# Attention's output projection by token halves, with five of its groups in the last slots of attention, and gating by halves

## The chip, the cores and the metric

One core of a Trainium2 chip runs the kernel. The metric is device time in microseconds (us) of one execution; the time before is a median of three runs.

## What is computed

Two transformer layers in fp32, on 1024 tokens of width 1024. The change lies in the first layer, between its attention and the product with `w_out`:

```
att = sliding_window_attention(aq, ak, av, sinks)          # (S, 512), 8 heads of 64
ret = retention_chunkwise(rq, rk, rv)                      # (S, 1024), 4 heads of 256
ret = head_group_norm(ret, gain) * silu(rg)                # "gating"
merged = sigmoid(ga) * (att @ w_att_o) + sigmoid(gr) * (ret @ w_ret_o)
x = x + merged @ w_out
```

## The kernel before

Each engine has a program of its own, written out by hand: `pe_program` (TensorE), `act_program` (ScalarE), `dve_program` (VectorE), `pool_program` (GpSimd), and a program of the SP queue that issues all DMAs. An engine works its instructions in that order; the order between engines comes from semaphores. Every fp32 operand of a large product is split in two parts, high (H) and low (L), and a product of 128 rows is three matmuls (WL by H, WH by L, WH by H; lines 597 to 599). Weights arrive in `WRAW` (three buffers), ScalarE writes the high part `WH`, VectorE or GpSimd the low part `WL` (lines 979, 1428, 2094), in seven slots. A weight tile is split in `feed(key)` once the last group that reads the slot's earlier tile is done, and SP fetches a tile once the one three before it has been split. The eight PSUM banks go round in the order in which TensorE opens them (`Banks.take`).

The stage has four parts.

1. The slot loop (line 776, 37 slots, s = 0 to 36). Retention has 32 turns `R1` (chunk t = 0 to 7, four heads), attention 32 turns `A1` (t = 0 to 7, four pairs of heads), each spread over several slots. TensorE's slot s holds, for attention turn a = s - 2: scores of a (line 749), values of a - 3 (line 761), the turning of the probabilities of a - 2 (line 772), and for retention scores of s, values of s - 1 (line 723), turning of s - 3 (line 738). Retention's turns end at slot 34, attention's scores at slot 33, its last values (turn 31) stand in slot 36. Between two steps of one turn the other engines work: VectorE adds the bias and takes the maximum (line 1602), ScalarE takes the exponential (1092), VectorE sums and inverts (1586, 1589), ScalarE and GpSimd scale, ScalarE copies the turned probabilities to `PT` (1112). The result of turn q goes to `ATH` (ScalarE, 1103) and `ATL` (VectorE, 1628), 128 features by 128 tokens. Tokens 0 to 511 (half 0) are complete with turn 15, tokens 512 to 1023 (half 1) with turn 31.
2. `ao`, attention's output projection (lines 791 to 794): 16 groups (n, half), n = 0 to 7 feature tiles, half = 0, 1 token halves, 12 matmuls of 128x512 each, ordered (0,0), (0,1), (1,0), ... It starts after the last turn's ATL. VectorE multiplies a group by its gate `TA` into `TB` (line 1645) and SP stores that to DRAM (2615).
3. The gating, one step beside each `ao` group: VectorE multiplies retention's output in `QK` by gain and gate `RG` (1638), ScalarE writes its high part `RH` (1132), GpSimd its low part `RL` (2212). SP loads the gates (2600, 2603).
4. `ro2`, retention's output projection (`RO2`, line 466), 16 groups of 24 matmuls. TensorE waits for RL of (7, half) before a group of that half. VectorE multiplies by the second gate and adds the stored `ao` group, both loaded in `MG` (2625, 2626; 1655, 1658). Then comes `out`, the product with `w_out`.

Of the kernel before, what the change touches and what calls it, by code (L numbers as in the profile page):

```python
# [147 lines left out]
def build(nc, a, out):  # L148
# [75 lines left out]
    TA = at("TA", [P, 2, S], MI + 18)  # L224
    RG = at("RG", [P, 4, 512], MI + 9.5)
    TB = at("TB", [P, 2, 512], MI + 5.5)
# [218 lines left out]

    def queries_in(t):

        return c.at(("lg0", "lg1", "lm0", "lm0")[t] if t < 4 else "lm1", "aq")
# [13 lines left out]
    LAG_A = 2  # L462
    A2 = [(h, i) for h in range(8) for i in range(NT)]
    OPEN = [(j, 0, 256) for j in range(4)] + [(j, 256, 256) for j in range(4)] + [(j, 512, 512) for j in range(4)]

    RO2 = [(n, half) for n in range(6) for half in range(2)] + [(n, half) for half in range(2) for n in range(6, 8)]
# [114 lines left out]
    def pe_program(e):  # L581
# [192 lines left out]

        nr, n1 = len(R1), len(A1)
        for s in range(n1 + LAG_A + 3):
            a = s - LAG_A
            if s < nr:
                ret_scores(s)
            if 0 <= a < n1:  # L780
                att_scores(a)
            if 0 <= s - 1 < nr:
                ret_values(s - 1)
            if 0 <= a - 3 < n1:
                att_values(a - 3)
            if 0 <= a - 2 < n1:
                att_turn(a - 2)
            if 0 <= s - 3 < nr:
                ret_turn(s - 3)

        w.wait_ge(*bk.out(("apv", n1 - 1)))
        for n in range(8):
            for half in range(2):
                proj_t(("ao", n, half), U["u_ao", n // 2], half, ATH, ATL, 4, (n % 2) * 512)
# [165 lines left out]
    def act_program(e):  # L960
# [168 lines left out]
        for i in range(16):  # L1129
            j, half = i // 2, i % 2  # L1130
            w.wait_ge(*c.at("rg_m", i))
            e.activation(RH[:, j, hs(half)], QK[:, j, hs(half)], ACT.Copy).then_inc(*c.inc("rg_h", (j, half)))
            feed(("ao", j, half))
# [283 lines left out]
    def dve_program(e):  # L1417
# [140 lines left out]

        nr, n1 = len(R1), len(A1)
# [4 lines left out]
        for s in range(n1 + LAG_A + 3):  # L1564
# [59 lines left out]
            if 0 <= q < n1:  # L1624
# [4 lines left out]
                                ATH[:, 2 * g + jp, blk(t)].bitcast(F32), ALU.subtract).then_inc(*bk.free(key))  # L1629
            if s == 3:  # L1630
                feed(("P3", 0, NB0 - 1, 0))
# [3 lines left out]
        for i in range(16):  # L1635
            n, half = i // 2, i % 2
            w.wait_ge(*c.at(f"lga{i % 4}", ("rg", i)))
            e.scalar_tensor_tensor(out=QK[:, n, hs(half)], in0=QK[:, n, hs(half)], scalar=GAIN[:, n:n + 1],
                                   in1=RG[:, i % 4, :], op0=ALU.mult, op1=ALU.mult).then_inc(*c.inc("rg_m", i))
            key = "ao", n, half  # L1640
            w.wait_ge(*bk.full(key))
            w.wait_ge(*c.at(f"lg{n % 2}", ("ga", n)))
            if i >= 2:
                w.wait_ge(*c.at(f"m1_{i % 2}", i - 2))
            e.tensor_tensor(TB[:, i % 2, :], PS[:, bk.at(key), :], TA[:, n % 2, hs(half)],
                            ALU.mult).then_inc(*bk.free(key))
            feed(key)
# [435 lines left out]
    def pool_program(e):  # L2083
# [125 lines left out]
        for i in range(16):  # L2209
            j, half = i // 2, i % 2  # L2210
# [3 lines left out]
            feed(("ao", j, half))  # L2214
# [215 lines left out]
    def sync_program(e):  # L2430
# [168 lines left out]
        def load_ga(n):  # L2599
            e.dma_start(TA[:, n % 2, :], scr_gx[n]).then_inc(*c.inc(f"lg{n % 2}", ("ga", n), 16))  # L2600

        def load_rg(i):
            e.dma_start(RG[:, i % 4, :], scr_rg[i // 2][:, hs(i % 2)]).then_inc(*c.inc(f"lga{i % 4}", ("rg", i), 16))

        stored0(NB0 - 1)
        w.wait_ge(*bk.out(("ro", len(R1) - 1)))
        for i in range(4):
            load_rg(i)
        w.wait_ge(*bk.out(("as", len(A1) - 1)))
        for n in range(2):  # L2610
            load_ga(n)
        for i in range(16):
            n, half = i // 2, i % 2
            w.wait_ge(*bk.out(("ao", n, half)))
            e.dma_start(scr_ga[n][:, hs(half)], TB[:, i % 2, :]).then_inc(*c.inc(f"m1_{i % 2}", i, 16))
            if half == 1 and n + 2 < 8:
                load_ga(n + 2)
            if i + 4 < 16:
                w.wait_ge(*c.at("rg_m", i))
                load_rg(i + 4)  # L2620
            feed(("ao", n, half))
# [390 lines left out]
```

## Time and profile before

| | us |
|---|---|
| median of 3 runs | 2707.33 (2704.08 to 2710.63) |
| the profiled execution, its own time | 2689.97 |
| its span, first to last instruction | 2688.2 |
| the span less TensorE's busy time | 57.3 |
| slot loop | 496 to 647 |
| `ao` and gating | 647 to 690.6 |
| `ro2` | 690.6 to 777.7 |

Times within the span are those of one profiled execution, on a clock that starts with its first instruction. A row of a timeline gives the start, the time from the first start to the last end of the merged instructions, engine, line and operands; in brackets stands the idle time of the engine before it and what ended it. Matmuls overlap, so their cost is read from start to start. The granted clock of TensorE (PEclk) is a share of 2.4 GHz.

### The profile page before, as it was taken

The page shows a single profiled execution, that of the slowest core. Times are in us where ns is not written, and L with a number is a line of the kernel's source. Part 1 is how long each engine was busy: PE and PEld are TensorE (multiplying, and loading weights), DVE is VectorE, ACT ScalarE, POOL GpSimd, SP SyncE. Part 2 cuts the span into 40 slices and gives each one's busy share as a digit, 9 for nine tenths or more (in the row PEclk, how much of TensorE's full clock was granted, in tenths as well). Part 3 has the DMA queues.
Part 4 walks back from the last instruction along what each step waited for, and adds up shares of the span by engine and source line. Part 5 has one row for each costly group of instructions (what it writes and reads, how often), then busy time and mean ns, then how long its engine had stood idle before and what let it go on. Part 6 is the DMA issues. An engine that isn't in the chain of part 4 may idle for free.

```text
span 2688.2 us, 35515 instructions
## 1 busy us (share of the span) xinstructions
PE 2630.9 (98%) x13170; PEld 2205.8 (82%) x13170; DVE 1548.2 (58%) x2628; ACT 1027.8 (38%) x2053; POOL 1179.5 (44%) x936
## 2 busy tenths in 40 slices
PE   7999999899999999999999999999999999999998
PEld 7788888677888988888888778989988888878886
DVE  4325555575434644554698641167647666668787
ACT  4122333475212423332444531057634322244443
POOL 2347878344425655565231763334234444300205
PEclk9999999899999999999999999999999999999999
DMA  4545766803542222222753344233043333273524
GB/s 169 181 184 204 266 228 249 305 1 122 199 169 90 79 86 79 79 86 71 274 184 99 114 153 142 74 69 65 20 141 100 104 114 106 95 257 133 188 95 164
DMA packets 161993, 372.35 MB, mean 139 GB/s; under 512 B 21365, under 2 KB 41973, under 8 KB 158197
## 3 DMA queue, kind: packets, MB, share of 16 engines
q1 hardware_dynamic: 161822, 370.08, 40.2%
q8 instruction: 106, 1.74, 0.3%
q14 instruction: 65, 0.53, 0.1%
HBM read 267.94 MB, written 101.83 MB: 138 GB/s over the span
## 4 chain that ended last, share of the span: by engine, by line
PE 88%; DVE 4%; POOL 2%; DMA 2%; ACT 2%; issue 1%; SPq 0%; POOLq 0%; DVEq 0%; ACTq 0%
PE PS L696 12%; PE PS L698 12%; PE PS L699 12%; PE PS L829 5%; PE PS L830 5%; PE PS L831 5%; PE PS L613 4%; PE PS L615 4%; PE PS L614 4%; PE PS L930 3%; PE PS L597 3%; PE PS L598 3%; PE PS L599 3%; PE PS L908 1%; PE PS L749 1%
## 5 line engine op out<-in xcount | busy, mean ns | idle before, releaser
L2094 POOL TENSOR_TENSOR WL<-WRAW,WH 128x512 fp32r<-128x512 f32 (+1 forms) x149 | 253.0, 1698 | 395.0 <-ACT WH L979 395.0
L696 PE MATMUL PS<-HH,WL 128*128 128x512 f32 (+1 forms) x928 | 349.0, 376 | 5.3 <-DVE HS L1736 3.1
L699 PE MATMUL PS<-HH,WH 128*128 128x512 f32 (+1 forms) x928 | 347.7, 375 | 0.0
L698 PE MATMUL PS<-HL,WH 128*128 128x512 f32 (+1 forms) x928 | 347.7, 375 | 0.0
L1428 DVE TENSOR_TENSOR WL<-TS,WH 128x512 fp32r<-128x512 f32 x216 | 227.5, 1062 | 182.9 <-ACT WH L979 182.8
L829 PE MATMUL PS<-WH,DAL 128*128 128x512 f32 x756 | 295.7, 391 | 5.5 <-DVE WL L1694 5.5
L830 PE MATMUL PS<-WL,DAH 128*128 128x512 f32 x756 | 294.7, 390 | 0.0
L831 PE MATMUL PS<-WH,DAH 128*128 128x512 f32 x756 | 294.6, 390 | 0.0
L2280 POOL TENSOR_TENSOR X<-X,DV 128x512 f32<-128x512 f32 x56 | 90.1, 1634 | 357.9 <-DVE DV L1806 275.3
L979 ACT ACTIVATE WH<-TS 128x512 fp32r<-128x512 f32 x216 | 130.9, 623 | 199.5 <-POOL TS L2110 199.4
L696 PEld LDWEIGHTS PS<-HH,WL 128*128 128x128 f32 x928 | 174.8, 188 | 37.1 <-DVE HS L1736 3.3
L613 PE MATMUL PS<-WH,HL 128*128 128x512 f32 x512 | 203.2, 397 | 1.2 <-DVE HL L1973 0.9
L699 PEld LDWEIGHTS PS<-HH,WH 128*128 128x128 f32 x928 | 174.9, 188 | 31.3
L698 PEld LDWEIGHTS PS<-HL,WH 128*128 128x128 f32 x928 | 174.9, 188 | 31.1
L615 PE MATMUL PS<-WH,HH 128*128 128x512 f32 x512 | 200.2, 391 | 0.0
L2110 POOL TENSOR_TENSOR TS<-WRAW 128x512 f32<-128x512 f32 x108 | 144.8, 1341 | 126.3 <-issue 122.8
L614 PE MATMUL PS<-WL,HH 128*128 128x512 f32 x512 | 199.9, 390 | 0.0
L979 ACT ACTIVATE WH<-WRAW 128x512 fp32r<-128x512 f32 (+1 forms) x236 | 175.4, 756 | 56.3 <-PE PS L615 18.7
L1428 DVE TENSOR_TENSOR WL<-WRAW,WH 128x512 fp32r<-128x512 f32 (+1 forms) x87 | 112.3, 1291 | 109.5 <-ACT WH L979 109.4
L829 PEld LDWEIGHTS PS<-WH,DAL 128*128 128x128 f32 x756 | 142.3, 188 | 37.8 <-issue 5.8
L1694 DVE TENSOR_TENSOR WL<-WRAW,WH 128x512 fp32r<-128x512 f32 x189 | 155.2, 821 | 23.6 <-ACT WH L1174 23.6
L831 PEld LDWEIGHTS PS<-WH,DAH 128*128 128x128 f32 x756 | 142.3, 188 | 29.4
(366 smaller groups left out, 6145.1 us busy)
## 6 DMA issues: line engine op xcount, KB each, us to landing
WRAW<-in_u_f SPq DMA_DIRECT2D x56, 512.0 KB, 3.6
WRAW<-in_u_in SPq DMA_DIRECT2D x54, 512.0 KB, 4.4
WRAW<-scr_t SPq DMA_DIRECT2D x52, 512.0 KB, 3.7
scr_h<-HS SPq DMA_DIRECT2D x96, 256.0 KB, 2.2
WRAW<-in_u_gu SPq DMA_DIRECT2D x44, 512.0 KB, 3.5
scr_t<-TTa SPq DMA_DIRECT2D x19, 1024.0 KB, 4.4
WRAW<-in_u_out SPq DMA_DIRECT2D x24, 512.0 KB, 3.5
scr_x<-X SPq DMA_DIRECT2D x24, 512.0 KB, 5.0
```

Source lines behind the costliest of these rows:

```text
L613: e.matmul(PS[:, b, :], HL[:, k, ts], whole_slot(WH, n)[:, cs], start=(k == 0), stop=False)
L614: e.matmul(PS[:, b, :], HH[:, k, ts], whole_slot(WL, n)[:, cs], start=False, stop=False)
L615: mm = e.matmul(PS[:, b, :], HH[:, k, ts], whole_slot(WH, n)[:, cs], start=False, stop=(k == 7))
L696: e.matmul(PS[:, b, 0:wd], wl[:, blk(kk)], op_moving(q, kk, c0, wd, 0), start=(kk == 0), stop=False)
L698: e.matmul(PS[:, b, 0:wd], wh[:, blk(kk)], op_moving(q, kk, c0, wd, 1), start=False, stop=False)
L699: mm = e.matmul(PS[:, b, 0:wd], wh[:, blk(kk)], op_moving(q, kk, c0, wd, 0), start=False, stop=(kk == 3))
L829: e.matmul(dst, hl, wh, start=(i == 0), stop=False)
L830: e.matmul(dst, hh, wl, start=False, stop=False)
L831: mm = e.matmul(dst, hh, wh, start=False, stop=(i == g - 1))
L979: e.activation(dst, src, ACT.Copy).then_inc(*c.inc("w_hi", i))
L1428: e.tensor_tensor(lo, raw, hi.bitcast(F32), ALU.subtract).then_inc(*c.inc("w_lo_v", i))
L2094: e.tensor_tensor(lo, raw, hi.bitcast(F32), ALU.subtract).then_inc(*c.inc("w_lo_p", i))
```

## The change

- `ao` is ordered by halves (`AOG`): all eight n of half 0, then all eight of half 1. Its first five groups (`N_TAIL` = 5), all of half 0, stand at the end of slots 32 to 36 of the slot loop, in TensorE's program and in VectorE's (the multiplication by the gate, after ATL). The other eleven follow the loop, after the same wait for the last ATL.
- The gating goes by halves too (`GATED`: j = 0 to 7 of half 0, then of half 1), still 16 steps; the first eleven stand beside `ao` groups 5 to 15, the last five alone.
- `ro2` takes n = 0 to 5 of half 0, then n = 0 to 5 of half 1 (before: both halves of each n); its last four groups are as before.
- The gate tiles of `ao` are now eight buffers of one half each: four in the place of `RV`'s chunks 4 and 5, loaded once retention's turn 23 is done, four in the place of `TA`. SP loads them one per group (16 of 256 KB, before 8 of 512 KB). Two of `RG`'s four buffers and `TB` lie in other places, and SP's loads of `RG` and its waits follow from that.

```diff
--- before.py
+++ after.py
@@ -221,9 +221,10 @@
     SM = at("SM", [P, 256], MI + 0.5)
     AB = at("AB", [P, 8, 256], MI + 18)
     FA = [at("FAa", [P, 512], MI + 13.5), at("FAb", [P, 512], MI + 15.5)]
-    TA = at("TA", [P, 2, S], MI + 18)
-    RG = at("RG", [P, 4, 512], MI + 9.5)
-    TB = at("TB", [P, 2, 512], MI + 5.5)
+    TA = ([at(f"TAa{i}", [P, 512], B2 + 16 + 2 * i) for i in range(4)]
+          + [at(f"TAb{i}", [P, 512], MI + 18 + 2 * i) for i in range(4)])
+    RG = [at(f"RG{i}", [P, 512], MI + kb) for i, kb in enumerate((9.5, 11.5, 1.5, 3.5))]
+    TB = at("TB", [P, 2, 512], MI + 13.5)
     MG = at("MG", [P, 2, 2, 512], MI + 1.5)
     RKN = at("RKN", [P, 2, P], MI + 1.5)
     STM = at("STM", [P, 2, P], MI + 2.5)
@@ -443,6 +444,13 @@
         base, scr = {0: (14, scr_qk), 1: (6, scr_gx), 2: (22, scr_rg), 3: (30, scr_gr)}[m // 4]
         return scr[tile - base][:, hs(int(q[0]) - 1)]
 
+    def gate_at(i):
+
+        return TA[i if i < 4 else 4 + i % 4]
+
+    def gate_in(i):
+        return c.at(("lg0", "lg1", "lm0", "lm1")[i % 4], ("ga", i))
+
     def queries_in(t):
 
         return c.at(("lg0", "lg1", "lm0", "lm0")[t] if t < 4 else "lm1", "aq")
@@ -460,10 +468,13 @@
     A1 = [(t, g, jp) for t in range(NT) for g in range(2) for jp in range(2)]
     R1 = [(t, h) for t in range(NT) for h in range(4)]
     LAG_A = 2
+    N_TAIL = LAG_A + 3
+    AOG = [(n, half) for half in range(2) for n in range(8)]
     A2 = [(h, i) for h in range(8) for i in range(NT)]
     OPEN = [(j, 0, 256) for j in range(4)] + [(j, 256, 256) for j in range(4)] + [(j, 512, 512) for j in range(4)]
 
-    RO2 = [(n, half) for n in range(6) for half in range(2)] + [(n, half) for half in range(2) for n in range(6, 8)]
+    GATED = [(j, half) for half in range(2) for j in range(8)]
+    RO2 = [(n, half) for half in range(2) for n in range(6)] + [(n, half) for half in range(2) for n in range(6, 8)]
     PO = [0, 4, 1, 5, 2, 6, 3, 7]
     OUTS = ([(0, tt) for tt in PO[:4]] + [(1, tt) for tt in PO[:4]] + [(1, tt) for tt in PO[4:]]
             + [(0, tt) for tt in PO[4:]])
@@ -772,6 +783,11 @@
                     mm = e.transpose(PS[:, b, blk(2 * e2 + kb)], PB[:, q % 3, e2, blk(kb)], ID[:, :])
             mm.then_inc(*bk.fill(("at", q)))
 
+        def att_out(i):
+            n, half = AOG[i]
+            w.wait_ge(*bk.out(("apv", n1 - 1 if half else n1 // 2 - 1)))
+            proj_t(("ao", n, half), U["u_ao", n // 2], half, ATH, ATL, 4, (n % 2) * 512)
+
         nr, n1 = len(R1), len(A1)
         for s in range(n1 + LAG_A + 3):
             a = s - LAG_A
@@ -787,11 +803,12 @@
                 att_turn(a - 2)
             if 0 <= s - 3 < nr:
                 ret_turn(s - 3)
+            if s >= n1:
+                att_out(s - n1)
 
         w.wait_ge(*bk.out(("apv", n1 - 1)))
-        for n in range(8):
-            for half in range(2):
-                proj_t(("ao", n, half), U["u_ao", n // 2], half, ATH, ATL, 4, (n % 2) * 512)
+        for i in range(N_TAIL, 16):
+            att_out(i)
         for n, half in RO2:
             w.wait_ge(*c.at("rg_l", (7, half)))
             proj_t(("ro2", n, half), U["u_ro", n], half, RH, RL)
@@ -1127,10 +1144,11 @@
 
         w.wait_ge(*bk.out(("ro", nr - 1)))
         for i in range(16):
-            j, half = i // 2, i % 2
+            j, half = GATED[i]
             w.wait_ge(*c.at("rg_m", i))
             e.activation(RH[:, j, hs(half)], QK[:, j, hs(half)], ACT.Copy).then_inc(*c.inc("rg_h", (j, half)))
-            feed(("ao", j, half))
+            if i + N_TAIL < 16:
+                feed(("ao", *AOG[i + N_TAIL]))
         for i, (n, half) in enumerate(RO2):
             w.wait_ge(*c.at("mg_a", i))
             e.activation(HH[:, n, hs(half)], MR[:, i % 2, :], ACT.Copy).then_inc(*c.inc("mg_h", (n, half)))
@@ -1555,6 +1573,18 @@
                     n_split[0] += 1
                 else:
                     feed(BEHIND[key][0])
+
+        def att_out(i):
+
+            key = "ao", *AOG[i]
+            w.wait_ge(*bk.full(key))
+            w.wait_ge(*gate_in(i))
+            if i < 2:
+                w.wait_ge(*bk.out(("rs", nr - 1)))
+                w.wait_ge(*c.at("r_q", nr - 1))
+            else:
+                w.wait_ge(*c.at(f"m1_{i % 2}", i - 2))
+            e.tensor_tensor(TB[:, i % 2, :], PS[:, bk.at(key), :], gate_at(i)[:, :], ALU.mult).then_inc(*bk.free(key))
 
         nr, n1 = len(R1), len(A1)
         w.wait_ge(*c.at("small", "all"))
@@ -1627,24 +1657,21 @@
                 w.wait_ge(*c.at("a_hi", q))
                 e.tensor_tensor(ATL[:, 2 * g + jp, blk(t)], PS[:, bk.at(key), 0:128],
                                 ATH[:, 2 * g + jp, blk(t)].bitcast(F32), ALU.subtract).then_inc(*bk.free(key))
+            if s >= n1:
+                att_out(s - n1)
             if s == 3:
                 feed(("P3", 0, NB0 - 1, 0))
 
         w.wait_ge(*bk.out(("rot", nr - 1)))
         w.wait_ge(*bk.full(("apv", n1 - 1)))
         for i in range(16):
-            n, half = i // 2, i % 2
+            n, half = GATED[i]
             w.wait_ge(*c.at(f"lga{i % 4}", ("rg", i)))
             e.scalar_tensor_tensor(out=QK[:, n, hs(half)], in0=QK[:, n, hs(half)], scalar=GAIN[:, n:n + 1],
-                                   in1=RG[:, i % 4, :], op0=ALU.mult, op1=ALU.mult).then_inc(*c.inc("rg_m", i))
-            key = "ao", n, half
-            w.wait_ge(*bk.full(key))
-            w.wait_ge(*c.at(f"lg{n % 2}", ("ga", n)))
-            if i >= 2:
-                w.wait_ge(*c.at(f"m1_{i % 2}", i - 2))
-            e.tensor_tensor(TB[:, i % 2, :], PS[:, bk.at(key), :], TA[:, n % 2, hs(half)],
-                            ALU.mult).then_inc(*bk.free(key))
-            feed(key)
+                                   in1=RG[i % 4][:, :], op0=ALU.mult, op1=ALU.mult).then_inc(*c.inc("rg_m", i))
+            if i + N_TAIL < 16:
+                att_out(i + N_TAIL)
+                feed(("ao", *AOG[i + N_TAIL]))
         for i, (n, half) in enumerate(RO2):
             key = "ro2", n, half
             w.wait_ge(*bk.full(key))
@@ -2207,11 +2234,12 @@
                 feed(("P3", 0, NB0 - 1, 0))
 
         for i in range(16):
-            j, half = i // 2, i % 2
+            j, half = GATED[i]
             w.wait_ge(*c.at("rg_h", (j, half)))
             e.tensor_tensor(RL[:, j, hs(half)], QK[:, j, hs(half)], RH[:, j, hs(half)].bitcast(F32),
                             ALU.subtract).then_inc(*c.inc("rg_l", (j, half)))
-            feed(("ao", j, half))
+            if i + N_TAIL < 16:
+                feed(("ao", *AOG[i + N_TAIL]))
         for i, (n, half) in enumerate(RO2):
             w.wait_ge(*c.at("mg_h", (n, half)))
             e.tensor_tensor(HL[:, n, hs(half)], MR[:, i % 2, :], HH[:, n, hs(half)].bitcast(F32),
@@ -2596,29 +2624,44 @@
             load_rv(t)
         feed(("P3", 0, NB0 - 1, 0))
 
-        def load_ga(n):
-            e.dma_start(TA[:, n % 2, :], scr_gx[n]).then_inc(*c.inc(f"lg{n % 2}", ("ga", n), 16))
+        def load_ga(i):
+            n, half = AOG[i]
+            e.dma_start(gate_at(i)[:, :], scr_gx[n][:, hs(half)]).then_inc(
+                *c.inc(("lg0", "lg1", "lm0", "lm1")[i % 4], ("ga", i), 16))
 
         def load_rg(i):
-            e.dma_start(RG[:, i % 4, :], scr_rg[i // 2][:, hs(i % 2)]).then_inc(*c.inc(f"lga{i % 4}", ("rg", i), 16))
-
+            j, half = GATED[i]
+            e.dma_start(RG[i % 4][:, :], scr_rg[j][:, hs(half)]).then_inc(*c.inc(f"lga{i % 4}", ("rg", i), 16))
+
+        nr, n1 = len(R1), len(A1)
         stored0(NB0 - 1)
-        w.wait_ge(*bk.out(("ro", len(R1) - 1)))
+        w.wait_ge(*bk.full(("ro", 4 * 5 + 3)))
+        w.wait_ge(*bk.full(("rst", 4 * 5 + 3)))
         for i in range(4):
-            load_rg(i)
-        w.wait_ge(*bk.out(("as", len(A1) - 1)))
-        for n in range(2):
-            load_ga(n)
+            load_ga(i)
         for i in range(16):
-            n, half = i // 2, i % 2
+            if i == 1:
+                w.wait_ge(*bk.full(("ro", nr - 1)))
+                load_rg(0)
+                load_rg(1)
+            if i == 3:
+                w.wait_ge(*bk.full(("rot", nr - 1)))
+                load_rg(2)
+                load_rg(3)
+            n, half = AOG[i]
             w.wait_ge(*bk.out(("ao", n, half)))
             e.dma_start(scr_ga[n][:, hs(half)], TB[:, i % 2, :]).then_inc(*c.inc(f"m1_{i % 2}", i, 16))
-            if half == 1 and n + 2 < 8:
-                load_ga(n + 2)
             if i + 4 < 16:
-                w.wait_ge(*c.at("rg_m", i))
-                load_rg(i + 4)
-            feed(("ao", n, half))
+                w.wait_ge(*bk.out(("as", n1 - 1)))
+                load_ga(i + 4)
+            if i >= N_TAIL:
+                if i - N_TAIL + 4 < 16:
+                    w.wait_ge(*c.at("rg_m", i - N_TAIL))
+                    load_rg(i - N_TAIL + 4)
+                feed(("ao", n, half))
+        for i in range(16 - N_TAIL, 12):
+            w.wait_ge(*c.at("rg_m", i))
+            load_rg(i + 4)
 
         def load_mg(i):
             n, half = RO2[i]
```

## Rows read from the trace of the kernel before

**Rows 1.** The page: span, and busy time of each engine with its share.

```profile
span 2688.2 us, 35515 instructions
PE 2630.9 (98%) x13170; PEld 2205.8 (82%) x13170; DVE 1548.2 (58%) x2628; ACT 1027.8 (38%) x2053; POOL 1179.5 (44%) x936
```

**Rows 2.** Busy time by stretch: length, five engines, PEclk, DMA share, GB/s.

```profile
600.00:630.00 30.00, 30.00 (x194) 21.89 (x193) 21.35 (x82) 23.17 (x81) 15.21 (x29) 1.00 0.01 2
637.20:647.00 9.80, 5.88 (x54) 4.12 (x53) 3.31 (x15) 6.52 (x21) 3.00 (x4) 1.00 0.63 214
647.00:690.60 43.60, 43.60 (x192) 36.12 (x193) 26.90 (x33) 12.74 (x19) 23.24 (x16) 1.00 0.79 268
690.60:720.00 29.40, 29.40 (x131) 24.34 (x130) 9.43 (x12) 6.35 (x9) 11.63 (x7) 1.00 0.49 163
...
750.00:777.00 27.00, 27.00 (x121) 22.34 (x120) 8.39 (x11) 5.07 (x7) 8.80 (x6) 1.00 0.37 117
```

**Rows 3.** Timeline of TensorE, slots 33 to 36 and the first `ao` matmul.

```profile
637.15 1.13 PE L749 MATMUL PS<-AK,AQ 64*128 64x256 f32 x4
...
639.29 0.38 PE L738 MATMUL PS<-ID,ON 128*128 128x128 f32 x2
641.56 0.66 PE L761 MATMUL PS<-PTb,AV 128*64 128x128 f32 x8 [1.88 <-ACT PTb L1112]
...
642.64 0.38 PE L738 MATMUL PS<-ID,ON 128*128 128x128 f32 x2
643.59 0.66 PE L761 MATMUL PS<-PTa,AV 128*64 128x128 f32 x8 [0.56 <-ACT PTa L1112]
644.18 0.66 PE L772 MATMUL PS<-ID,PB 128*128 128x128 f32 x4
645.61 0.66 PE L761 MATMUL PS<-PTb,AV 128*64 128x128 f32 x8 [0.78 <-ACT PTb L1112]
646.97 0.50 PE L597 MATMUL PS<-ATH,WL 128*128 128x512 f32 x1 [0.69 <-DVE ATL L1628]
```

**Rows 4.** Timeline of TensorE, second `ao` matmul, and where `ro2` begins.

```profile
647.31 0.39 PE L598 MATMUL PS<-ATL,WH 128*128 128x512 f32 x1
...
690.63 0.39 PE L597 MATMUL PS<-RH,WL 128*128 128x512 f32 x1
```

**Rows 5.** Timeline of VectorE and ScalarE around slot 33, and VectorE's first gate product.

```profile
637.62 0.54 DVE L1580 TENSOR_SCALAR ON<-PS,RS 128x256 f32<-128x256 f32 x1
638.79 0.48 DVE L1602 CUSTOM_DVE_ANT_0 PB<-PS,AB,SM 128x256 f32<-128x256 f32 x1
...
650.03 0.69 DVE L1645 TENSOR_TENSOR TB<-PS,TA 128x512 f32<-128x512 f32 x1 [2.45 <-PE PS L599]
```

**Rows 6.** Groups by line, 647 to 690.6 (POOL, DVE, ACT): count | busy, mean ns.

```profile
L2212 POOL TENSOR_TENSOR RL<-QK,RH 128x512 fp32r<-128x512 f32 x15 | 20.5, 1374 | 24.1 <-ACT RH L1132 24.1
L2094 POOL TENSOR_TENSOR WL<-WRAW,WH 128x1024 fp32r<-128x1024 f32 x1 | 2.9, 2857 | 0.0
...
L1645 DVE TENSOR_TENSOR TB<-PS,TA 128x512 f32<-128x512 f32 x15 | 10.4, 690 | 15.4 <-PE PS L599 11.0 <-DMA scr_m<-TB 4.4
L1428 DVE TENSOR_TENSOR WL<-WRAW,WH 128x1024 fp32r<-128x1024 f32 x2 | 2.7, 1348 | 1.1 <-ACT WH L979 1.1
...
L1132 ACT ACTIVATE RH<-QK 128x512 fp32r<-128x512 f32 x16 | 10.1, 633 | 30.5 <-DVE QK L1638 30.5
L979 ACT ACTIVATE WH<-WRAW 128x1024 fp32r<-128x1024 f32 x3 | 3.2, 1056 | 0.8 <-PE PS L599 0.7
```

**Rows 7.** Tile RG: the gating product (min/median/max ns), and its loads' time to landing.

```profile
L1638 DVE SCALAR_TENSOR_TENSOR QK<-QK,SM,RG x16: 735/744/1805, 646.8 to 689.4; 128x512 f32<-128x512 f32 x16
...
DMA to landing us min/median/max: 2.8/4.4/6.1
```

**Rows 8.** Tile MG: `ro2`'s first product (first and last start), and its waits.

```profile
L1655 DVE TENSOR_TENSOR MR<-PS,MG x16: 691/692/693, 700.3 to 777.9; 128x512 f32<-128x512 f32 x16
...
DMA MG<-scr_m: 8.8, 1
```

## The prediction, made before the changed kernel was run

> **What bounds the kernel now.** I read the page first: TensorE is busy 2630.9 us of a span of 2688.2, so all that it does not do at once is 57.3 us [rows 1]. Then the stretches around the change: TensorE is busy for the whole of each from 600 to 777 us, at granted clock 1.00, but for one, 637.2 to 647.0, where it is busy 5.88 of 9.80 us [rows 2]. Its timeline names that idle time: 1.88, 0.56 and 0.78 us before the values of slots 34, 35 and 36, each ended by ScalarE's copy of the turned probabilities, and 0.69 us before the first `ao` matmul, ended by ATL of the last turn [rows 3]. Together 3.91 us. These slots hold only what drains: a few small matmuls and the way round the other engines. After them `ao` and `ro2` run without an idle moment, 16 groups of `ao` in 690.63 - 646.97 = 43.66 us, 2.73 us each [rows 3, 4].
>
> So TensorE bounds this stage, and a change can give back here at most the 3.91 us in the drain.
>
> **Part by part.**
>
> *Five groups into the drain.* No matmul is added or removed: 16 groups of 12 before and after. Five groups are 5 x 2.73 = 13.6 us of work put between the small steps. Half 0 needs turns 0 to 15 only, done long before, and the weights of `ao` are split near the loop's start. I lay TensorE's queue out. Slot 32 ends where the scores of slot 33 began, 637.15 [rows 3]. Group 0 runs to 639.9. The small matmuls of slot 33 took 637.15 to 639.67 (2.5 us), those of slot 34 641.56 to 643.02 (1.5), those of slot 35 643.59 to 644.84 (1.25), those of slot 36 645.61 to 646.27 (0.66) [rows 3]. That gives: slot 33 to 642.4, group 1 to 645.1; slot 34 to 646.6, group 2 to 649.3; slot 35 to 650.6, group 3 to 653.3; slot 36 to 654.0, group 4 to 656.7; then eleven groups, 30.0 us, to 686.7. Before it was 690.63. The difference is the 3.91 us, if no group makes a new wait.
>
> *What the groups push back on the other engines.* VectorE's product with the gate stands in its queue after ATL and waits for the whole group; behind it wait the next slot's normalisation, sum and maximum, and for these ScalarE's exponential and PT copy, and for that the next values on TensorE. Slot 33 is the tight one, as it still has a maximum to take. A gate product started 3.06 us after its group's first matmul (650.03 against 646.97) and takes 0.69 [rows 3, 5], so it is done at 637.15 + 3.06 + 0.69 = 640.9. From the start of the normalisation to the end of the second maximum VectorE took 637.62 to 639.27, 1.65 us [rows 5]: done at 642.55. From there to the values of slot 34 the old trace took 641.56 - 639.27 = 2.29 us [rows 3, 5], so they can start at 644.85. TensorE's queue reaches them at 645.1. A cover of 0.25 us: free by my count, and if the count is off, a stall of some tenths. Without that cover the delay of the chain, 3.3 us, would be seen in full; it is hidden by group 1. The later slots have no maximum, and group 2 or 3 (2.73 us) lies ahead of each values step, against ways round of 0.6 to 0.8 us more than TensorE's own work [rows 3]: hidden. The last ATL now has group 4 before its reader, so its 0.69 us goes too. PSUM banks return after eight openings; the closest is the turning of slot 33, which needs the bank that the normalisation of the same slot frees at about 641.4, and TensorE is there at about 642.2.
>
> *The price of alternating.* No row shows a large group between small ones. From below: nothing. From above, two rows: the first matmul of `ao` was 0.34 us ahead of the second where later ones are 0.227 apart (43.66 / 192), a head of 0.11 us [rows 3, 4]; five heads in place of one cost 0.45. The way back, from a group to small matmuls, has no row; as the same head, twice as dear, it would be 4 x 0.23 = 0.9. A gain below nothing is excluded, since nothing is taken away but waits. I take 0.45, as the head is a row of these very instructions, and keep 0 to 1.4.
>
> *Gating by halves.* Its instructions are the same in number and size. It starts after group 4's product, at about 657.7 instead of 646.8, and goes one step a group. `ro2` then asks at 686.7 for RL of (7, 0), the eighth step. Step 7 stands in VectorE's queue behind the product of group 11 (group's end 656.7 + 7 x 2.73 = 675.8, plus the lag of 0.33 and 0.69: 676.8). Then 0.74 for the step [rows 7], 0.63 for RH and 1.37 for RL [rows 6]: 679.5. Two weight splits come in between, as a tile of `w_att_o` now comes free only with its group of half 1: `w_ret_o` tile 3 after group 9 (ScalarE 1.06, VectorE 1.35), which the two groups' slack takes up, and tile 4 after group 11 (ScalarE 1.06, GpSimd 2.86) [rows 6]. Both the latter stand before RH and RL of step 7, so RL comes at 676.1 + 1.06 + 0.63 of RH of step 6 + 2.86 + 1.37 = 682.0 to 682.5. TensorE asks at 686.7: a cover of some 4 us, nothing paid.
>
> *The tail of the gating.* The last five steps run after `ao`. SP's last RG load waits behind the store of group 15 and the fetch that needs tile 6 split (group 15's end 686.7, then 1.06 + 0.63 + 1.37 + 2.86, about 692.5). Landing takes 4.4 us [rows 7], so step 15 is at 697 and the MG loads, which wait for it, land near 702.5, against 700.3 for the first product before [rows 8]. `ro2`'s first group is full at 692.2, so two groups lie in PSUM while six banks are free: nothing on TensorE, which before passed 9 us of the same waiting of VectorE without a gap [rows 2, 8]. RL of (7, 1) is wanted at 686.7 + 6 x 5.44 = 719 and comes near 700.
>
> *`ro2` by halves.* The groups of `ro2` take 5.44 us each (sixteen from 690.6 to 777.7). A new tile is wanted every 5.44 us instead of every 10.9 for the first six. Tiles 0 to 2 are there before; 3, 4, 5 are asked for at 703, 708 and 714 and are split by 673, 681 and 684. Tile 7's slot comes free after `ro2` group 6 (724.8) and is wanted at 757; the first `w_out` tiles' slots after groups 7 to 10, 730 to 747, and are wanted at 773.8. All hidden.
>
> *SP and DMA.* Eight more gate loads of half the size, two issues of 0.43 us and a store of 0.32 in each 2.73 us; the bytes are the same. Four of the loads now fall where DMA is at 0.01 [rows 2]. No cost. The stretch of `ao` and gating had a DMA share of 0.79 and is now shorter by 10 us with some of its loads ahead of it.
>
> **The sum.** 3.91 - 0.45 = 3.5 us less. The profiled execution took 2689.97, with 1.8 us around its span; it would be 2686.5 (span 2684.7). It lies 17.4 us under the median of the runs, so I carry the difference over, not the ratio: 2707.33 - 3.5 = 2703.8 us. Ends: 3.9 with no price, 2.3 with heads both ways and 0.3 of stall in slot 33.
>
> **Rivals.**
>
> 1. *The waits stay, in new places.* VectorE's queue makes TensorE wait in slots 33 to 35. The cover of 0.25 us in slot 33 speaks for it, the 2.73 us in the others against. If every slot lost 0.6 us, 2 to 3 us of the gain would go: about 2706.5.
> 2. *Slower: `ro2` waits for the gating's eighth step.* Its low part comes 4.2 us before TensorE asks, and every us beyond that is lost. The mechanism is there: the gating product took 0.74 us alone but up to 1.81 beside GpSimd [rows 7], 1.07 more. If each of the steps 0 to 7 lost that one after the other, 8.6 us, RL would be at 690.9, 4.2 us late, and the time 2708.0, slower than before. Slower by over 0.2%, 2712.8, needs another 4.8 us, for instance the two weight splits of 2.86 and 1.35 us delayed as much again, and some 13 us in all against my count. Against it: steps wait for groups and so take up delay between them. It decides from 4.2 us on.
>    The Trainium skill, "SBUF — State Buffer", section "Who interferes with whom", says of VectorE and GpSimd that the pair of ports they share is an exclusive lock, and that a VectorE instruction with two SBUF inputs contends with a GpSimd one that reads SBUF. By that rule each such product could wait for a whole RL of 1.37 us or a split of 2.86; the spread of the rows agrees with a lock. Where it would hold for each step in turn, the time would be rival 2's 2708 or up to 2 us more.
> 3. *It does more than it says.* Small matmuls of slots 33 to 36 count as busy but may hide idle time that full queues take up; at most one slot's worth, 2.5 us: 2701.3.
>
> **Chances.** Forecast (gain 2.3 to 4.2): 0.60. Rival 1: 0.18. Rival 2 or a wait like it: 0.12. Rival 3: 0.10. A measurement of this kernel can tell about 0.2%, 5.4 us, from no change, and the forecast lies under that; runs of one kernel alone spread by 6.5 us. So within 0.2%: nearly all of the forecast and of rival 1, half of the others, and a little of each goes over the bound by the spread: 0.74. Faster by over 0.2%: 0.14. Slower: 0.12. The range takes in all four cases with half the spread of the runs: 2698.5 to 2710.
>
> **What would show it.** Right: no idle time of TensorE over 0.3 us between 637 and 657; the first `ro2` matmul 3 to 4 us earlier, near 687; RL's eighth start before 682; the first MR product near 702 with TensorE busy throughout. Wrong: a bracket before a values step (rival 1), a bracket "DVE" or "POOL" before the first RH matmul or before a weight tile's first use in `ro2` (rival 2), or any new wait between 720 and 778. If the stage ends 3.5 us earlier and the time does not follow, the difference is in stages that the change does not touch.

## The result: 0.3% faster, more than twice what was forecast

| | us |
|---|---|
| before, median of 20 runs | 2704.19 (2690.17 to 2715.18) |
| after, median of 20 runs | 2694.61 (2686.51 to 2705.81) |
| ratio | 0.9970, 95% interval 0.9957 to 0.9984 |
| profiled execution, before | 2689.97 |
| profiled execution, after | 2701.57 |

The change saves 0.3%, some 8 us, with an interval of 4 to 12. Forecast were 3.5 us, and 2698.5 us as the lower end. The forecast stood on a median of three runs before, 2707.33; that of twenty is 3.1 us lower, and this part of the distance from 2703.8 to 2694.61 is no gain of the change. The two profiled executions point the other way: that of after is 11.6 us the longer. So the first thing to find is where that profile lost time, and the second why the runs gained more than the idle time of the drain.

**The stage of the change.** Stretches of the changed kernel, whose span is 2699.8 us (same columns as [rows 2]):

```profile
637.40:657.50 20.10, 20.10 (x118) 15.39 (x117) 6.05 (x19) 6.81 (x23) 3.34 (x4) 1.00 0.48 157
657.50:687.10 29.60, 29.60 (x132) 24.53 (x131) 17.27 (x23) 9.40 (x13) 15.04 (x11) 1.00 0.85 276
687.10:720.00 32.90, 32.90 (x146) 27.24 (x146) 16.91 (x18) 7.80 (x12) 19.56 (x13) 1.00 0.54 184
```

TensorE has no idle time left where [rows 2] had 3.9 us, and none behind it. Its timeline in the slots, matmuls of the groups left out but for first and last:

```profile
637.43 0.38 PE L749 MATMUL PS<-ID,ON 128*128 128x128 f32 x2
637.57 0.48 PE L608 MATMUL PS<-ATH,WL 128*128 128x512 f32 x1
...
640.48 1.13 PE L760 MATMUL PS<-AK,AQ 64*128 64x256 f32 x4
...
642.62 0.38 PE L749 MATMUL PS<-ID,ON 128*128 128x128 f32 x2
642.76 0.47 PE L608 MATMUL PS<-ATH,WL 128*128 128x512 f32 x1
...
645.38 0.39 PE L610 MATMUL PS<-ATH,WH 128*128 128x512 f32 x1
645.70 0.66 PE L772 MATMUL PS<-PTb,AV 128*64 128x128 f32 x8
```

The values of slot 34 (645.70) follow group 1 with no bracket. I measure the stage by its way: from the start of the last matmul of retention scores (both operands in `QK`) to the first matmul of `ro2`, and call it the way. That is 629.8 to 690.6 before, 60.8 us, and 630.4 to 687.2 after, 56.8 us: 4.0 us less.

**The rest of the profile.** From the first `ro2` matmul to the end of the span it is 1997.6 us before (2688.2 - 690.6) and 2012.6 after (2699.8 - 687.2), though no instruction there has changed. The stretch at the start of the second layer's attention shows it, before and then after:

```profile
1762.00:1790.00 28.00, 26.94 (x201) 23.39 (x200) 17.86 (x69) 17.30 (x41) 11.99 (x11) 1.00 0.48 91
```

```profile
1762.00:1790.00 28.00, 27.58 (x119) 22.87 (x119) 9.68 (x38) 8.88 (x22) 6.15 (x6) 0.57 0.34 58
```

In 28 us TensorE did 201 matmuls before and 119 after, at a granted clock of 0.57: most of that stretch at 1.2 GHz, the lower of the clock's two levels (0.50). (The same point of the work comes 2.6 us earlier in the second.) It begins where both traces have the same gap:

```profile
1765.04 1.30 PE L930 MATMUL PS<-V,PT 128*128 128x64 f32 x10 [1.06 <-DVE PT L1981]
```

```profile
1762.42 1.66 PE L947 MATMUL PS<-V,PT 128*128 128x64 f32 x10 [1.06 <-DVE PT L2008]
```

The first is of before, the second of after; the ten matmuls behind the gap took 1.30 and 1.66 us. The granted clock of after is 0.50 from 1763.2 to 1787.1, from 0.8 us behind the gap on. So a drop of the clock can follow this gap and need not, and one execution does not tell which. The 20 runs of after lie in two heaps, 2686.5 to 2693 (ten) and 2696 to 2706 (ten); those of before in no such order, and one alone below 2694.

### The profile page after: what moved, and what is told of

The parts are those of the page before. It is cut to its first block, busy times and chain, and to the rows that moved or that the text cites. A ratio compares the mean times of both kernels' runs of the same rounds, so it can differ in the third digit from the quotient of the medians.

```text
span 2699.8 us, 35526 instructions
## 1 busy us (share of the span) xinstructions
PE 2643.6 (98%) x13170; PEld 2215.7 (82%) x13170; DVE 1551.0 (57%) x2628; ACT 1027.2 (38%) x2053; POOL 1180.4 (44%) x936
## 4 chain that ended last, share of the span: by engine, by line
PE 89%; DVE 4%; POOL 2%; DMA 2%; issue 2%; ACT 1%; SPq 0%; POOLq 0%; DVEq 0%; ACTq 0%
PE PS L707 12%; PE PS L710 12%; PE PS L709 12%; PE PS L846 5%; PE PS L848 5%; PE PS L847 5%; PE PS L624 4%; PE PS L626 4%; PE PS L625 4%; PE PS L947 3%; PE PS L608 3%; PE PS L609 3%; PE PS L610 3%; PE PS L925 1%; PE PS L760 1%
```

## The experiments

"Way" is the stage as above; "rest" is the time from the first `ro2` matmul to the end of the span; "clock" says where the trace of that kernel shows 1.2 GHz, in the drain (D) or at the second attention (A). Left out are three drops that all traces have (at 500 to 527, at 2390 to 2417 and at the end of the span; the first comes with two waits for DMA of 3.4 and 3.5 us) and short ones, of 3 to 7 us, that only some have (near 17, 97, 1556, 1964 and from 2059 to 2085).

| run | way | rest | clock | median (lowest to highest), runs | ratio to before |
|---|---|---|---|---|---|
| before | 60.8 | 1997.6 | none | 2704.19 (2690.17 to 2715.18), 20 | 1 |
| f0b, before again | 60.8 | 2013.2 | A | 2704.78, one | |
| after | 56.8 | 2012.6 | A | 2694.61 (2686.51 to 2705.81), 20 | 0.9970 (0.9957 to 0.9984) |
| e1, after again | 56.8 | 2013.6 | A | 2699.67 (2686.41 to 2705.11), 12 | 0.9973 (0.9954 to 0.9992) |
| e2, after + 4.1 us | 60.9 | 2011.2 | A | 2691.13 (2688.77 to 2703.70), 12 | 0.9967 (0.9949 to 0.9986) |
| e3, before - 4.1 us | 60.8 | 2003.1 | at 690 | 2707.04 (2696.26 to 2712.90), 12 | 1.0012 (0.9999 to 1.0026) |
| e4, halves alone | 65.8 | 2012.4 | D, A | 2704.36 (2695.02 to 2714.98), 12 | 0.9995 (0.9977 to 1.0012) |
| f1b, before, drain filled | 60.6 | 2010.5 | A | 2697.17 (2688.94 to 2705.19), 12 | 0.9970 (0.9950 to 0.9990) |
| f2b, first gap filled | 60.8 | 1997.5 | none | 2696.77 (2689.15 to 2708.24), 12 | 0.9971 (0.9952 to 0.9990) |
| g1b, after, A filled | 56.7 | 1997.8 | none | 2687.39 (2685.32 to 2693.80), 6 | 0.9940 (0.9921 to 0.9959) |
| h1, before, A filled | 65.8 | 2002.4 | D | 2695.37 (2690.20 to 2700.27), 11 | 0.9970 (0.9959 to 0.9981) |
| h2, before, both filled | 60.6 | 1997.4 | none | 2691.21 (2689.63 to 2694.13), 5 | 0.9952 (0.9934 to 0.9970) |
| h3 = g1b again | 56.8 | 1997.1 | none | 2686.88 (2684.78 to 2689.08), 5 | 0.9936 (0.9920 to 0.9951) |
| h4, three groups | 58.3 | 2011.0 | A | 2702.36, one | |

The ratios stand to the kernel before as it ran beside them: a median of 2704.36 (35 runs) beside e1 to e4, of 2705.34 (23) beside the f runs and g1b, and of 2705.34 (15) beside the h runs. Labels with a b are second attempts; the first ones (f0, f1, f2, g1) gave no result.

### Is it the shift in time? (e1 to e4)

Three theories T, L and S of the extra gain are put up with e1: that a shift by 4 us changes how many executions meet the drop at the second attention, that this share was luck, and that the change saves 8 us in every run.

**e1** is the changed kernel unedited.

> The changed kernel once more, nothing edited. The traces so far: the stretch from slot 32 of the first attention to the first matmul of ro2 is 4.06 us shorter than before (56.99 to 52.94), and the profiled run of the changed kernel had a stretch at half the clock near 1765 to 1788 us, at the start of the second layer's attention, which the profiled run of the kernel before did not have; it cost about 10.5 us there. The twenty runs of the changed kernel lie in two heaps, near 2688 and near 2700. Theory T (timing): the gain is 4 us in every run, and the rest of the 8 to 9.6 us comes from that clock drop being met in a smaller share of the runs when everything after ro2 comes 4 us earlier; expects two heaps again, about half the runs in the low one, median 7 to 10 us under before. Theory L (luck): the share of runs with the drop does not depend on the kernel; expects the same share as before in the same call, and a median 4 us under it. Theory S (steady): the change saves 8 us in every run; expects the low heap of before to lie 8 us over the low heap of this one.

**e2** puts the 4 us back as work. In `proj_t`:

```diff
             w.wait_ge(*lo_done(OPU[n]))
+            for _ in range(18 if key == ('ao', 7, 1) else 0):
+                e.matmul(PS[:, b, :], whole_slot(WH, n)[:, 0:128], h[:, 0, hs(half)], start=True, stop=True)
             for k in range(nk):
```

> The changed kernel with 18 extra 128x512 matmuls ahead of the last ao group, 18 x 0.227 = 4.1 us of TensorE, as much as the drain gave back; ro2 and all behind it start when they do in the kernel before. Theory T: like the kernel before in every way, ratio 1.000, few runs in the low heap. Theory L: ratio 1.000 as well, the same share of runs in each heap as all kernels of this call. Theory S (something beyond the drain saves 4 us more, by halves or by the loads): 4 us less than before.

**e3** takes 18 matmuls out of the kernel before; its `ao` groups (7, 0), (7, 1) and a quarter of (6, 1) lack their low parts.

```diff
+                cut = key in (("ao", 7, 0), ("ao", 7, 1)) or (key == ("ao", 6, 1) and k == 3)
+                if not cut:
-                e.matmul(PS[:, b, :], wl, h[:, k, hs(half)], start=(k == 0), stop=False)
-                e.matmul(PS[:, b, :], wh, l[:, k, hs(half)], start=False, stop=False)
+                    e.matmul(PS[:, b, :], wl, h[:, k, hs(half)], start=(k == 0), stop=False)
+                    e.matmul(PS[:, b, :], wh, l[:, k, hs(half)], start=False, stop=False)
-                mm = e.matmul(PS[:, b, :], wh, h[:, k, hs(half)], start=False, stop=(k == nk - 1))
+                mm = e.matmul(PS[:, b, :], wh, h[:, k, hs(half)], start=(k == 0 and cut), stop=(k == nk - 1))
```

> The kernel before with 18 of the 192 ao matmuls left out (the two products with low parts, of groups (7,0) and (7,1), and of the last quarter of (6,1)), 4.1 us of TensorE; order, gating and loads are those of before, the drain idles as before, and ro2 with all behind it starts 4.1 us earlier. Theory T: the same as the changed kernel: two heaps, about half the runs in the low one, 7 to 10 us under before. Theory L: 4 us under before, heaps as before. Theory S: 4 us under before, and 4 us slower than the changed kernel.

**e4** is the change without its groups in the slots. The same two lines go from VectorE's program, and SP issues the first four `RG` loads ahead of the stores of `ao`.

```diff
-    N_TAIL = LAG_A + 3
+    N_TAIL = 0
...
-            if s >= n1:
-                att_out(s - n1)
```

> The change without its five groups in the last slots (N_TAIL 0): ao, gating and ro2 by halves, the new places of the gates, all 16 ao groups after the loop; SP loads the first four RG halves ahead of the ao stores. From slot 32 to the first matmul of ro2 57.0 us as before (the drain idles 3.9 us). Theories T and L: same as before, ratio 1.000. Theory S, if the order by halves is what saves: 4 us less.

e1 repeats the result and the two heaps (four runs up to 2690.9, eight from 2698.9). e2 refutes theory T as I had it: with way and positions of the kernel before, it is not like that kernel but 0.33% faster, its low heap near 2690.5 with seven of twelve runs. What it shares with after and not with before is a drain without idle time. It is no plain case for theory S either: its low heap lies 2 to 3 us over that of after, where the 4 us of padding belong. e4 speaks against the order by halves as the source of the 8 us: ratio 0.9995, and 0.9970 lies outside its interval. The 4 us of theory S, 0.9985, lie within it; against these speaks that its way, 65.8, is that of h1, the old order with the same drop of the clock.

e3 is flawed, and of use all the same. The way did not get shorter: the last group was done 4 us sooner, and then `ro2` waited 3.9 us for RL of (7, 0). In the old order of the gating that step is the fifteenth of sixteen and had no cover to speak of; the new order is what lets `ro2` start earlier. And the clock fell in that wait: it is 0.50 from 689.5 to 696.4, and 0.68 over ten us:

```profile
691.43 0.80 PE L599 MATMUL PS<-RH,WL 128*128 128x512 f32 x1 [3.91 <-POOL RL L2214]
```

```profile
690.00:700.00 10.00, 8.57 (x28) 6.87 (x29) 1.95 (x3) 1.58 (x2) 5.00 (x4) 0.68 0.36 121
```

The trace of e4 has what the first trace of before lacked. Its drain, with a gap of 1.89 us where [rows 3] have 1.88, and all small matmuls behind it at nearly twice their time:

```profile
639.62 0.38 PE L749 MATMUL PS<-ID,ON 128*128 128x128 f32 x2
641.89 1.13 PE L772 MATMUL PS<-PTb,AV 128*64 128x128 f32 x8 [1.89 <-ACT PTb L1127]
642.95 1.12 PE L783 MATMUL PS<-ID,PB 128*128 128x128 f32 x4
...
649.62 0.79 PE L608 MATMUL PS<-ATH,WL 128*128 128x512 f32 x1 [0.69 <-DVE ATL L1656]
650.21 0.63 PE L609 MATMUL PS<-ATL,WH 128*128 128x512 f32 x1
```

```profile
640.00:645.00 5.00, 2.76 (x17) 2.08 (x18) 0.82 (x4) 3.56 (x13) 0.92 (x1) 0.67 0.00 0
645.00:650.00 5.00, 3.53 (x21) 2.42 (x21) 1.02 (x3) 1.15 (x3) 0.00 (x0) 0.50 0.33 108
650.00:655.00 5.00, 5.00 (x13) 3.84 (x13) 0.23 (x1) 0.63 (x1) 1.27 (x1) 0.50 0.00 0
```

Matmuls of `ao` come 0.43 us apart (650.21 to 650.64 and on) where they came 0.227 apart in [rows 4]. The way is 65.8 us instead of 60.8: this drop cost 5.0 us. The clock is 0.50 from 641.66 to 655.3; it fell when TensorE had been idle for 1.66 of the 1.89 us. The granted clock of TensorE is the second price of the drain, beside the idle time: I call it theory D. The Trainium skill, "TensorE: Matmul & The Clock Gate", section "HAM oscillation — how this bites in real kernels", tells of it for a thin matrix product: gaps between bursts of matmuls throttle the array again, and each next burst starts at the lower clock. The traces here agree in kind, in some executions and not in all, with gaps as short as 1.89 and 1.06 us.

### Is it the clock in the drain? (f0b to f2b)

**f0b** is the kernel before, looked at once more.

> The kernel before once more, for a second trace of it. The trace of the kernel with halves alone (e4) shows the granted clock at half for 13.65 us from 641.9 on, right in the drain, and its runs lie where those of before lie, while no trace of the changed kernel shows it. Theory D (drain clock): most runs of the kernel before have such a stretch, and its first profile, at 2690 us, was one of the rare runs without; expects a stretch at half clock between 640 and 660 here and a time of 2695 or more. Theory T (only the position of the second attention matters): granted clock 1.00 from 540 to 1750.

**f1b** leaves the kernel before as it is and fills its gaps with matmuls that nobody needs; **f2b** fills the first gap alone (`{29: 8}`, nothing at `ao`). In f1b `proj_t` takes the bank `first` for group (0, 0) in place of opening one.

```diff
+        def spin(b, count):
+            for _ in range(count):
+                w.wait_ge(*lo_done(OPU[U["u_ao", 0]]))
+                e.matmul(PS[:, b, :], whole_slot(WH, U["u_ao", 0])[:, 0:128], ATH[:, 0, hs(0)], start=True, stop=True)
...
             b = open_bank(("apv", q))
+            spin(b, {29: 8, 30: 2, 31: 3}.get(q, 0))
             w.wait_ge(*bk.out(("at", q)))
...
+        first = open_bank(("ao", 0, 0))
+        spin(first, 3)
         w.wait_ge(*bk.out(("apv", n1 - 1)))
```

> The kernel before with 16 extra 128x512 matmuls, whose results are overwritten, in the four gaps of the drain: 8 before the values of slot 34, 2 of slot 35, 3 of slot 36, 3 before the first ao group (16 x 0.227 = 3.6 us in 3.9 us of idle time). No work is moved, nothing ends earlier by itself. Theory D: no stretch at half clock after the drain, so 4 to 5 us less than before; its lowest runs near 2690 to 2691 where those of before are near 2695. Theory T, and every account in which only the 4 us of moved work count: the same as before, or some tenths of a us more.

> The same with the first gap alone filled (8 matmuls in the 1.88 us before the values of slot 34); gaps of 0.56, 0.78 and 0.69 us stay. Theory D, if it is the long gap that lets the clock fall: as f1b, 4 to 5 us less than before. Theory D, if the sum of the gaps counts: between f1b and before. Theory T: the same as before.

f0b is a miss: the clock is 1.00 from 540 to 1750, and its 2704.78 us come from a drop at the second attention (rest 2013.2). So not every execution of before has the drop in the drain. The timed runs decide: f1b does no work less than before and is 0.30% faster, as fast as the whole change; its lowest runs are at 2688.9 to 2692 (six of twelve), where 78 runs of before in these three comparisons have one. Theories that count only moved work are out. f2b gives the same with the first gap alone filled, the others of 0.56, 0.78 and 0.69 us still in its trace: as far as twelve runs tell, the gap of 1.88 us is the one that matters. f1b's trace has no idle time and no drop in the drain, where e4's had 0.67 in these 5 us:

```profile
639.89 2.09 PE L756 MATMUL PS<-ATH,WH 128*128 128x512 f32 x8
641.93 0.66 PE L767 MATMUL PS<-PTb,AV 128*64 128x128 f32 x8
```

```profile
640.00:645.00 5.00, 5.00 (x39) 3.58 (x38) 0.91 (x5) 3.97 (x14) 0.93 (x1) 1.00 0.88 293
```

The traces alone would not show it, as a drop need not come: of five with the gap of 1.9 us two have it (e4, h1), of nine without that gap none.

### The second place, and the sum (g1b to h4)

**g1b** and **h3** are the changed kernel, **h1** the kernel before, **h2** that of f1b, each with one product in the gap of 1.06 us:

```diff
                 b = open_bank(("pv", q))
+                if q == 0:
+                    for _ in range(1):
+                        e.matmul(PS[:, b, :], ID[:, :], Q2[:, 2, 0:512], start=True, stop=True)
                 w.wait_ge(*c.at("vr", 7))
```

> The changed kernel with one extra fp32 product of 128x512 (two matmuls, about 0.9 us) in the second layer's attention, in the 1.06 us gap before its first values, where the half clock of the changed kernel's profile begins. Theory: that gap, as the drain's, lets the clock fall, and it makes the two heaps near 2688 and 2700; filled, all runs lie near 2688 and the median is 5 to 11 us under that of the changed kernel. Rival: the clock falls there because of the small 64-row matmuls around it; then two heaps as before, median 2690 to 2700.

> The kernel before with the one extra product in the gap of the second layer's attention, as in g1b; the drain of the first is as before. So far: the drop of the clock at the second attention costs 13 to 16 us after ro2's start (1997.6 us without, 2010.5 to 2013.6 with), one in the drain 5.0 us (e4). Theory D: this removes the drops at the second attention and leaves those of the drain, so two heaps, 2690 without and near 2696 with, the second the larger; median 8 to 10 us under before. Rival (the fill in the drain and the one here act on the same thing): all runs near 2690.

> The kernel before with both fills: no gap in the drain and none at the second attention, no work moved. Theory D: one heap near 2690.5, 3 to 6 us under h1. It is the kernel before without either drop, and against h3 it gives the plain worth of the change: 4.0 us by the stage in the traces.

> The changed kernel with the fill at the second attention, a second time. One heap near 2687, 3 to 4 us under h2; 17 us under before.

In all four the runs beyond 2700.3 are gone. h1 misses in part: its median is 10 us under before, as said, but its eleven runs are spread from 2690 to 2700 and form no two heaps. The gap of h3, where the clock fell in e1, now reads:

```profile
1761.27 0.38 PE L933 MATMUL PS<-K,Q 64*128 64x64 f32 x2
1761.58 1.12 PE L944 MATMUL PS<-Q,ID 128*128 128x512 f32 x2
1762.56 1.30 PE L950 MATMUL PS<-V,PT 128*128 128x64 f32 x10
```

```profile
1762.00:1790.00 28.00, 28.00 (x213) 24.72 (x212) 17.29 (x64) 16.71 (x40) 11.49 (x11) 1.00 0.42 74
```

213 matmuls in those 28 us, against 119. Of ten traces without this product seven have the drop, of four with it none; it costs 13 to 16 us of the rest (2010.5 to 2013.6 against 1997.1 to 1997.8). Where it lasted 23.9 us a second one of 3.4 to 6.8 us came near 1961 to 1965 (five of the seven; in the two others it lasted 30.7 us), and no trace without the first has the second: its price is in those 13 to 16 us. The rest of h1, 2002.4, holds an idle wait of 3.8 us up to 1555.0, for VectorE's `HLF`, and a drop of 3.4 us behind it; no other trace waits there for more than 1.0 us, and why this one did stays open.

With the second place quiet the change can be taken apart by medians: h1 2695.4, h2 2691.2, h3 2686.9. Filling the drain is worth 4.2 us (h1 to h2), ending it 4.0 us sooner by the way, 4.3 by the runs (h2 to h3), together 8.5, where the plain comparison has 8. These medians stand on eleven, five and five runs. And the plain comparisons do not split that way: there f1b's fill alone gives 8 us and the shorter way adds nothing to it. Their intervals are some 5 us either way, which covers it; a share of the second drop that hangs on the drain would make it too (see what is left open). h1's own trace has the drop in the drain, again with a way of 65.8 us and again behind a gap of 1.89:

```profile
641.91 1.13 PE L761 MATMUL PS<-PTb,AV 128*64 128x128 f32 x8 [1.89 <-ACT PTb L1115]
```

h3 and g1b are 0.6% faster than before and beat the changed kernel by 7 to 13 us (2687.4 and 2686.9 against 2694.6 and 2699.7); as a version to keep, it is the changed kernel plus one product whose result is overwritten.

**h4** asks whether the waits fall one by one, as the prediction laid them out: `N_TAIL = 3`, and `att_out` only in slots 32 to 34.

> The changed kernel with three groups in the slots (32 to 34) in place of five, the other thirteen after the loop; loads, gating and order of halves as in the change. By the layout of TensorE's queue the gaps of 1.88 and 0.56 us are filled and those before the values of slot 36 and before the first later ao group, 0.78 and 0.69 us, stay: the way from the last retention scores to ro2's first matmul 58.3 us, against 60.8 before and 56.8 with five groups.

The way is 58.3 us, to the tenth, and these two waits are left of the four in [rows 3]:

```profile
PE PS L772 <- ACT PTb L1129: 0.8, 1, 0.8
PE PS L608 <- DVE ATL L1658: 0.7, 1, 0.7
```

## Why the prediction was wrong

**The bound failed.** That "a change can give back here at most the 3.91 us in the drain" counted idle time alone. Idle time in a stretch of TensorE has a second price, the clock of the work behind it, and I took that for nothing since [rows 2] show 1.00 in the drain. They come from one execution. e4 and h1 show the drop, 5.0 us each; f1b shows that removing it without moving any work is worth as much as the whole change in plain comparison, and h1 against h2 that it is 4.2 us at the median. Of the 9.2 us between the forecast of 2703.8 and the median of 2694.61, 3.1 are the median of before that came down with more runs, some 4 the clock of the drain, and 0.5 the price of alternating that did not come; the rest, 1.4, is within the spread. The same kernel had a median of 2699.67 in e1, within the range forecast, as a median between two heaps moves easily; its ratio, 0.9973, was the same.

**The sign was in the numbers.** The profiled execution lay 17.4 us under the median of the runs, and I carried the difference over without asking what makes one kernel's runs differ by 17 us. 2690 is the kernel before without either drop (h2: 2689.6 to 2694.1); with that at the second attention it took 2704.8 (f0b), and e4, which has both, 2710.1. What I called the spread of the runs was for the most part such drops (20 runs of before spread by 25.0 us, five each of h2 and h3 by 4.5 and 4.3), and the part that starts in the drain belonged to the change.

**The sum of the drain** was right but for its price of alternating. 3.91 us were found, 0.45 taken off, 3.5 forecast; the way fell by 4.0. The head of a group is there (642.76 to 643.07, 0.31 us), but the group's first matmul starts while the last small one still drains (637.43 and 637.57), which a wait does not allow; the trace shows no net price. The layout held to some tenths once the 0.59 us by which the slots came later in this trace are taken off: scores of slot 33 at 640.48 (laid out: 639.9), `ro2` at 687.16 (686.7). One figure was off and nothing hung on it: the stretch of the eleven groups is 30.0 us by the sum, so 13.7 us shorter than the 43.7 before, not 10.

**The slot with 0.25 us of cover** held. The second maximum was done at 642.84 and the values of slot 34 followed group 1. Rival 1 did not come.

**Rival 2** did not come. RL's eighth step, between two weight splits as foreseen:

```profile
677.66 2.84 POOL L2121 TENSOR_TENSOR WL<-WRAW,WH 128x1024 fp32r<-128x1024 f32 x1
680.46 1.30 POOL L2239 TENSOR_TENSOR RL<-QK,RH 128x512 fp32r<-128x512 f32 x1
```

It ends at 681.8 (forecast 682.0 to 682.5), 5.4 us ahead of `ro2`. The gating's tail was late by about as much as said: step 15 at 699.2 (697), the first product with MG at 704.1 (702.5), TensorE busy throughout. e3 shows what the old order would have done to an earlier end of `ao`: 3.9 us of waiting.

**Rival 3**, that the change does more than it says, has the right sign for the wrong reason. It was to be hidden idle time in the small matmuls, at most 2.5 us; what came on top was their rate in some executions, 4.2 us.

**Left open.** Why a drop follows a gap in some executions and not in others; and whether the drain has a say in how often the second attention drops. Of 32 runs of after (first comparison and e1) 18 lie in the upper heap, from 2696 on; of 78 of before 60 lie above 2700.8, where a drop at the second attention, or both drops, would put them. That is a larger share, but the heaps of before overlap. The mean granted clock that each timed run has sorts them a little better: it is 0.990 or less in 55 of the 73 runs of before beside the experiments, in 34 of 68 of the kernels with the gap of 1.9 us filled and that of 1.06 not (after, e1, e2, f1b, f2b), and in 2 of 27 with the second gap filled. This points to a say of the drain; it is no proof, as other drops can bring a run to 0.990 as well (h1's profiled one), and no experiment here parts the two.

## What to carry to other kernels

Before costing an idle gap of TensorE, compare the profiled execution with the median of the runs: if it is the faster by more than the change is worth, the profile lacks something that the runs have, and a second trace is due before the sum. A gap of one to two us among small matmuls may cost several times its length in clock; filling it, with real work or with a product that is thrown away, is worth trying first at the place with the longest gap. And an engine-bound stage is only moved forward if what its successor waits for is moved too, as the gating's order was here.

## What the runs showed of the hardware

- Gaps of 1.06 and 1.89 us were enough to be followed by 1.2 GHz: small matmuls at nearly twice their time, 128x512 ones 0.43 us apart instead of 0.227. In the drain the lower clock lasted 13.65 us and cost 5.0; at the second attention it lasted 23.9 or 30.7 us and cost 13 to 16, with the short second drop in it.
- It is a matter of the execution, not of the kernel alone: two traces of the same unedited kernel before had neither drop (2689.97 us) and one (2704.78).
- With a throwaway product in the gap of the second attention no trace of four had the drop, against seven of ten without it, and none of the 27 timed runs went beyond 2700.3. In the drain it was enough to fill the long gap alone.
